# Expert outputs scattered to their tokens' rows in memory and read back, in place of a product with a zero-one matrix

## The reference

```python
p_group = softmax(h @ router_group); pg_top, g_idx = top_k(p_group, 1)
# two best experts inside the chosen group, softmax over their logits
combine = sum(one_hot(expert_id, 16) * (pg_top * w_inner)[..., None], axis=2)
for e in range(16):
    hid = silu(h @ w_gate[e]) * (h @ w_up[e])        # 2048 -> 512
    y = y + combine[..., e:e + 1] * (hid @ w_down[e])  # 512 -> 2048
x = x + y
```

## Time and profile before

| | us |
|---|---|
| median of 3 runs | 2903.97 (2903.62 to 2904.36) |
| profiled execution, device time | 2903.89 |
| its span on the core | 2902.2 |
| PE / DVE / ACT / POOL busy | 2873.0 / 1944.2 / 1648.0 / 95.7 |
| mean DMA rate over the span | 219 GB/s |

### The profile page before, as it was taken

How to read it: one execution, slowest core, us unless ns; L and a number is a source line. 1 busy time by engine, 2 the same in 40 slices (tenths; PEclk the granted TensorE clock), 3 DMA queues, 4 the chain that set the end, 5 groups by cost and what they waited for, 6 DMA issues and landing times.

```text
span 2902.2 us, 40355 instructions
## 1 busy us (share of the span) xinstructions
PE 2873.0 (99%) x16476; PEld 2534.4 (87%) x16476; DVE 1944.2 (67%) x2249; ACT 1648.0 (57%) x1916; POOL 95.7 (3%) x80
## 2 busy tenths in 40 slices
PE   8999999999999999999999999999999999999998
PEld 8989988898778888888999988888899999888887
DVE  6767444535599999999675864555565678555556
ACT  6554444434588888887556544555545655344544
POOL 2212000000000000000000000000000000000000
PEclk9999999999999999999999999999999999999999
DMA  7545566645499999999555555555554545555555
GB/s 270 185 160 169 187 211 235 214 157 170 141 332 366 360 363 356 363 369 313 169 171 175 190 193 184 189 180 182 192 194 156 193 160 187 196 193 181 189 194 189
DMA packets 282103, 636.66 MB, mean 219 GB/s; under 512 B 19081, under 2 KB 32962, under 8 KB 264642
## 3 DMA queue, kind: packets, MB, share of 16 engines
q1 hardware_dynamic: 280450, 628.86, 63.0%
q10 hardware_dynamic: 1184, 4.20, 0.4%
q0 software_dynamic: 288, 1.05, 0.1%
HBM read 626.72 MB, written 7.36 MB: 218 GB/s over the span
## 4 chain that ended last, share of the span: by engine, by line
PE 94%; DVE 3%; ACT 1%; issue 1%; DMA 0%; SPq 0%; POOL 0%; POOLq 0%; ACTq 0%; DVEq 0%
PE pairs L741 16%; PE pairs L743 16%; PE pairs L742 16%; PE pairs L761 10%; PE pairs L763 10%; PE pairs L765 10%; PE pairs L1118 2%; PE pairs L1120 2%; PE pairs L1119 2%; DVE w_lo L2089 2%; PE misc L1236 2%; ACT w_hi L1473 1%; PE misc L908 1%; DVE b_lo L2615 1%; PE misc L981 0%
## 5 line engine op out<-in xcount | busy, mean ns | idle before, releaser
L2089 DVE TENSOR_TENSOR w_lo<-raw,w_hi 128x1024 fp32r<-128x1024 f32 x1072 | 1308.6, 1240 | 796.9 <-ACT w_hi L1473 789.6
L1473 ACT ACTIVATE w_hi<-raw 128x1024 fp32r<-128x1024 f32 x1072 | 1122.3, 1061 | 940.5 <-PE pairs L743 547.2
L761 PE MATMUL pairs<-a_hi,w_hi 128*128 128x256 f32 x1920 | 549.0, 286 | 1.5 <-DVE w_lo L2089 1.5
L763 PE MATMUL pairs<-a_lo,w_hi 128*128 128x256 f32 x1920 | 544.0, 283 | 0.0
L765 PE MATMUL pairs<-a_hi,w_lo 128*128 128x256 f32 x1920 | 544.0, 283 | 0.0
L741 PE MATMUL pairs<-w_hi,a_hi 128*128 128x512 f32 x1280 | 504.7, 394 | 3.6 <-DVE w_lo L2089 1.6
L743 PE MATMUL pairs<-w_hi,a_lo 128*128 128x512 f32 x1280 | 498.5, 389 | 0.0
L742 PE MATMUL pairs<-w_lo,a_hi 128*128 128x512 f32 x1280 | 498.4, 389 | 0.0
L761 PEld LDWEIGHTS pairs<-a_hi,w_hi 128*128 128x128 f32 x1920 | 369.2, 192 | 3.9 <-issue 1.9
L763 PEld LDWEIGHTS pairs<-a_lo,w_hi 128*128 128x128 f32 x1920 | 369.3, 192 | 0.5
L765 PEld LDWEIGHTS pairs<-a_hi,w_lo 128*128 128x128 f32 x1920 | 369.1, 192 | 0.0
(11 more groups left out here) (387 smaller groups left out, 3043.0 us busy)
## 6 DMA issues: line engine op xcount, KB each, us to landing
raw<-in_w_in_dram SPq DMA_DIRECT2D x232, 1024.0 KB, 5.1
raw<-in_w_out_dram SPq DMA_DIRECT2D x84, 1024.0 KB, 5.1
raw<-in_w_down_dram SPq DMA_DIRECT2D x54, 1024.0 KB, 6.2
raw<-in_w_gate_dram SPq DMA_DIRECT2D x51, 1024.0 KB, 5.9
raw<-in_w_up_dram SPq DMA_DIRECT2D x51, 1024.0 KB, 6.7
raw<-in_xattn_wk_dram SPq DMA_DIRECT2D x16, 1024.0 KB, 5.0
raw<-in_xattn_wv_dram SPq DMA_DIRECT2D x16, 1024.0 KB, 5.0
raw<-in_xattn_wq_dram SPq DMA_DIRECT2D x16, 1024.0 KB, 5.0
```

Of the source, the lines that this page charges most:

```text
L761: nc.tensor.matmul(o, w_hi[:, s, q, fs], hi[:, k, :], start=(k == 0 and f % 2 == 0), stop=False, skip_group_check=True)
L763: nc.tensor.matmul(o, w_hi[:, s, q, fs], lo[:, k, :], start=False, stop=False, skip_group_check=True)
L1473: a.activation(w_hi[:, h % HSLOTS], landing(h)[:, 2 * (h % 2):2 * (h % 2) + 2, :], ACT.Copy).then_inc(hi_done, 1)
L2089: v.tensor_tensor(w_lo[:, h % HSLOTS], landing(h)[:, 2 * (h % 2):2 * (h % 2) + 2, :], w_hi[:, h % HSLOTS].bitcast(F32), ALU.subtract).then ...
```

## The change

The product with `place` goes. GpSimd writes the rows of each down unit to memory, each slot's row to its token's row of `y_dram[n]` (one for each quarter n), and slots without a token get a row number past the bound and are dropped. All 256 rows of a quarter are complete after the last group's write. Then GpSimd reads the quarter back, in token order, and DVE adds it to `x` once for each quarter, not once for each group and quarter.

```diff
+        y_dram = [nc.dram_tensor(f"expert_rows{n}", (S + 1, COLS), F32).ap() for n in range(4)]
-        place = rounded("place", 512, [P, TT, S])
-        y_lo_r = rounded("y_low", 1024, [P, TT, COLS])
-        y_hi_r = rounded("y_high", 4608, [P, TT, COLS])
+        y_out = [sc(4608, TT, COLS), sc(1024, TT, COLS)]
+        y_back = sc(0, TT, COLS)
...
                 def turn_pick(g):
...
-                    for s in range(tiles):
+                    for s in range(TT):
                         for T in range(TT):
-                            nc.tensor.matmul(misc[:, 0, s * (PER_GROUP + 1):(s + 1) * (PER_GROUP + 1)],
-                                             pick[:, T, s * P:(s + 1) * P], comb[:, T, g, :],
-                                             start=T == 0, stop=T == TT - 1)
-                    for s in range(tiles):
-                        for T in range(TT):
-                            m = nc.tensor.transpose(misc[:, 1, s * S + T * P:s * S + (T + 1) * P],
-                                                    pick[:, T, s * P:(s + 1) * P], ident[:])
+                            m = nc.tensor.matmul(misc[:, 0, s * COMB:(s + 1) * COMB],
+                                                 pick[:, T, s * P:(s + 1) * P], comb[:, T, g, :],
+                                                 start=T == 0, stop=T == TT - 1)
...
-                def spread_y(g, n):
...
-                    for T in range(TT):
-                        for s in range(tiles):
-                            at = place[:, s, T * P:(T + 1) * P]
-                            nc.tensor.matmul(misc[:, 2 + T, :], at, y_hi_r[:, s, :], start=s == 0, stop=False)
-                            m = nc.tensor.matmul(misc[:, 2 + T, :], at, y_lo_r[:, s, :], start=False,
-                                                 stop=s == tiles - 1)
...
 # GpSimd
+            for gr in range(GROUPS):
+                pool.wait_ge(row_ok, gr + 1)
+                for n in range(4):
+                    sent = (y_even, y_odd)[n % 2]
+                    copied(pool, moe_u(gr, E0 + n))
+                    for T in range(TT):
+                        g.indirect_dma_start(y_dram[n], bass.IndirectOffsetOnAxis(ap=slot_row[gr % 2][:, T:T + 1], axis=0),
+                                             y_out[n % 2][:, T, :], None, bounds_check=S, oob_is_err=False)\
+                         .then_inc(sent, 16)
+                    if gr == GROUPS - 1:
+                        pool.wait_ge(sent, 32 * (2 * gr + n // 2 + 1))
+                        if n:
+                            pool.wait_ge(x_added, n)
+                        pool.dma_start(y_back, y_dram[n][1:S + 1].rearrange("(t p) c -> p t c", p=P))\
+                            .then_inc(y_read, 16)
...
 # ScalarE: place_copy is gone
             def y_copy(g, n):
 
                 done("moe", UNITS_G * g + E0 + n)
-                if 4 * g + n:
-                    act.wait_ge(spread, 4 * g + n)
-                a.activation(y_hi_r[:], pairs[:, n % 2], ACT.Copy).then_inc(y_hi_ok, 1)
+                if 4 * g + n >= 2:
+                    act.wait_ge((y_even, y_odd)[n % 2], 32 * ((4 * g + n) // 2))
+                a.activation(y_out[n % 2], pairs[:, n % 2], ACT.Copy).then_inc(pair_read[n % 2], 1)
...
 # VectorE: y_low is gone; combine() also multiplies the token's number into comb (one more small product)
+            def slot_rows(g):
...
+                s1(v.tensor_scalar(no_row, comb_slot[:, :, 5], 0.0, 4.0 * S, ALU.is_equal, ALU.mult))
+                v.tensor_tensor(slot_row[g % 2], no_row, comb_slot[:, :, 5], ALU.add).then_inc(row_ok, 1)
...
-            def add_spread(g, n):
+            def add_back(n):
 
-                dve.wait_ge(spread, 4 * g + n + 1)
+                dve.wait_ge(y_read, 16 * (n + 1))
                 xs = x[:, :, n * COLS:(n + 1) * COLS]
-                v.tensor_tensor(xs, misc[:, 2:4], xs, ALU.add).then_inc(x_added, 1)
+                v.tensor_tensor(xs, y_back, xs, ALU.add).then_inc(x_added, 1)
...
                     else:
-                        run(3); y_low(g, n - 1); run(1)
+                        run(4)
...
-                        run(3); add_spread(g, n - 1); run(1)
+                        run(4)
+                        if g == GROUPS - 1:
+                            add_back(n - 1)
```

More of the change, by code:

```diff
@@ L29 @@
 EXPERTS = GROUPS * PER_GROUP
+COMB = PER_GROUP + 2
 POOL_WINDOWS = (2, 4, 8, 16)
@@ L167, in program @@
         rsum = tiny(2)
-        comb = tiny(TT * GROUPS * (PER_GROUP + 1)).rearrange("p (t g e) -> p t g e", t=TT, g=GROUPS)
-        comb_slot = tiny(TT * (PER_GROUP + 1)).rearrange("p (t e) -> p t e", t=TT)
+        comb = tiny(TT * GROUPS * COMB).rearrange("p (t g e) -> p t g e", t=TT, g=GROUPS)
+        comb_slot = tiny(TT * COMB).rearrange("p (t e) -> p t e", t=TT)
+        token_i = tiny(TT).bitcast(I32)
+        token_f = tiny(TT)
+        no_row = tiny(TT)
+        slot_row = [tiny(TT).bitcast(I32) for _ in range(2)]
         sq_gain = tiny(8).rearrange("p (t j) -> p t j", t=TT)
@@ L385, in program @@
         hid_mm = sem("hid_mm")
-        y_hi_ok = sem("y_hi_ok")
-        spread = sem("spread")
+        y_odd = sem("y_odd")
+        y_read = sem("y_read")
         x_added = sem("x_added")
@@ L834, in turn_sum @@
                 if N == 4:
-                    pe.wait_ge(x_added, 4 * (GROUPS - 1) + c + 1)
+                    pe.wait_ge(x_added, c + 1)
                     pe.wait_ge(n_lo, n)
@@ L1203, in experts @@
                 unit(pc(U["lru0"]), H["lru0"], 0, mm_features, a_hi, a_lo, need=ready(4),
-                     hooks={1: lambda: spread_y(GROUPS - 1, 3), 3: lambda: turn_sum(4, 3, "moe")})
+                     hooks={3: lambda: turn_sum(4, 3, "moe")})
             route_last()
@@ L1832, in x_low @@
                         act.wait_ge(var_ok, 4)
-                        act.wait_ge(x_added, 4 * (GROUPS - 1) + 3)
+                        act.wait_ge(x_added, 3)
                     low_squares(x, T, junk_low, sq_part)
@@ L1849, in x_top @@
                 def x_top():
-                    act.wait_ge(x_added, 4 * GROUPS)
+                    act.wait_ge(x_added, 4)
                     top_squares(x[:, :, 3 * COLS:4 * COLS], sq_part)
@@ L2438, in _ @@
                     few_low()
-            dve.wait_ge(slots_in, 1)
+            dve.wait_ge(slots_in, 2)
+            v.tensor_copy(token_f, token_i)
             for i in range(4):
@@ L2644, in _ @@
                         if g:
-                            run(3); y_low(g - 1, 3); run(4)
-                            add_spread(g - 1, 3); run(1)
+                            run(8)
                         else:
@@ L2655, in _ @@
                             group_slots()
+                        slot_rows(g)
                     elif i == 2 and g < GROUPS - 1:
@@ L2680, in moe_rest @@
             def moe_rest():
-                y_low(GROUPS - 1, 3)
                 split_lo(4, 2, a_hi, a_lo, "norm0")
@@ L2687, in gained @@
                 dve.wait_ge(gain_in, 16)
-                dve.wait_ge(x_added, 4 * (GROUPS - 1) + j + 1)
+                dve.wait_ge(x_added, j + 1)
                 v.tensor_tensor(xg[j], x[:, :, j * COLS:(j + 1) * COLS],
@@ L2952, in _ @@
                         todo[3].append(moe_rest)
-                        todo[4].append(lambda: add_spread(GROUPS - 1, 3))
+                        todo[4].append(lambda: add_back(3))
                         todo[6].append(lambda: gained(3))
```

31 lines of the change are left out of this document (8 added, 23 removed).

## The result

The changed kernel takes 2908.4 us (median of 20 runs, 2904.7 to 2914.7), the kernel before 2903.7 beside it: ratio 1.0016, 95% interval 1.0010 to 1.0022. It is 4.7 us slower. That is inside what the prediction called no difference, but on the other side of 2903.7 than the forecast of 2901, and outside the 2896 to 2907 of its likeliest case. Eighteen of the runs of before lie within 1.2 us (2903.2 to 2904.4) and one at 2905.9, those of after spread over 10 us, which is itself a sign: their time hangs on something that varies. One run of before (6003.4 us) and one of e12_unawaited (3128.9 us) lie far outside and count in no median here.

The account below looks back on a forecast made before the run. It took TensorE as the bound, DVE and transfers near their limits. Groups 0 to 2 -7, last group's products -3.6, round trip +5.5, transfers +1.5, small DVE work +0.5: -3.1 from 2903.97, say 2901 us; range 2892 to 2912.

Parts of the forecast that it names:

- likeliest case: The forecast's own case: R 10 to 15, transfer ceiling near 372 GB/s; 2896 to 2907 us, chance 0.48.
- What goes: `spread_y` products at 16 places leave TensorE's path, 14.5 us; DVE additions, ACT copies and `turn_pick` buy nothing.
- Groups 0 to 2: Twelve places free 10.9 us of TensorE; a transfer ceiling of 372 GB/s lets 7 of it come home.
- Rival 1: Faster: 372 GB/s is demand, not ceiling, and R is about 11; 10 us gained, 2894 us, chance 0.31.
- A rule against the change: Expert stage: a limit of about 358 GB/s per core would make it transfer-bound already, longer by every byte added.
- The last group: Its four spreads give 3.6 us, but the round trip through memory counts there, as DVE waits in order.
- R: Time from the end of `y_copy` to the landing of the read-back: taken as 12.0 us, from 9.5 to 17.
- What R costs: Last group: first quarter late by R - 8.7, third R - 9.8, others hidden; together 2R - 18.5, 5.5 us.
- hidden unless R passes 13: Last group's fourth quarter: `lru0` turns it after four halves of 2.9 us, so only R above 13 costs.
- Transfers +1.5: Last group: reads and last writes, 2.6 MB, delay weights in flight by 1.5 us, bounds 0 and 4.
- Rivals 2 and 4: Slower: 361 GB/s is all there is, 2914 us; or dropped rows move too, about 2912; together chance 0.10.
- Rival 3: Slower by the round trip: GpSimd's indirect issues take 2 us or more, R = 17; +9, 2913 us, chance 0.11.

Follow-up runs that it names:

- e12_unawaited: Changed kernel with all its transfers, but DVE's addition replaced by a same-size instruction that waits for no read-back (experts' part left out of the output): 2892.5 us.
- e2_no_write: Changed kernel without indirect writes and read-backs, DVE's addition replaced by a same-size instruction without a wait (experts' part left out of the output): 2890.7 us.
- e7_more_traffic: e5_hybrid with one more transfer of 512 KB to memory at each of the 12 places of groups 0 to 2: 2899.9 us.
- e8_late: Changed kernel with the same transfers, but the last group's additions, turns and splits after a read-back stand later, for quarters 0 and 1 one unit: 2900.2 us.
- e5_hybrid: Changed kernel, but the last group keeps the product with the zero-one matrix; groups 0 to 2's rows are read back and added early: 2895.1 us, ratio 0.9971.
- e10_late_one: e8_late with only the first 128 slots of a place sent, one indirect transfer instead of two: 2899.7 us.
- e4_one_issue: Changed kernel with only the first 128 slots of a place sent, one indirect transfer instead of two: 2899.7 us.
- e3_fill: Changed kernel with 26 unused matmuls of 512 columns (5.9 us) before the turn of the last group's first quarter and of its fourth: 2912.2 us.
- e11_plain: Changed kernel, but in the last group each indirect transfer is a plain one of 128 rows, which do not reach their tokens: 2903.0 us.

## Why the prediction went wrong, point by point

- **What goes** (14.5 us of products, the rest worth nothing): right. e2_no_write, which removes them and adds no transfer, gives 13.0. The 1.5 missing may be the small DVE work (a term of 0.5) and weights that TensorE now overtakes: ACT waits 6.2 us for four of their loads there. No run separates the two.
- **Groups 0 to 2, "so I take 372 as the ceiling"**: wrong, 7 us where 10.4 came in this trace. A share of 1.02 does not say that no more can move: at 1.01 it was 388, in e7_more_traffic at 1.03 406. The failed step was to take the rate at a full share for a limit, where TensorE set the demand. Rival 1 had this part right.
- **A rule against the change** (about 358 GB/s): it did not bind, 375 over a group and 406 in a stretch. Another page of the Trainium skill (HBM Reference, section Specifications (TRN2)) says that a core that streams alone gets well above that share, about 425. The traces agree that it gets more; over 61 us the most that was asked for and moved is 406.
- **"The last group", R = 12**: this is the step that failed and that decides. The term was mis-sized: R was 16.6, 12.7 and 16.6 where it counts. Of the first's 4.6 us too many, the read is 2.3 (8.8 for 6.5), the write's landing 1.9 (4.73 for 2.6 + 0.2), the notice 0.5 (0.83 for 0.3), and the issues, where I had looked for the risk, -0.1 (2.26 for 2.4).
- **What R costs**: the formulas have the right places, and give too little. With the measured values the first quarter gives 16.6 - 8.7 = 7.9, the third 12.7 - 9.8 = 2.9, the fourth 16.6 - 13 = 3.6 and the second nothing: 14.4. These R are of the profiled execution of after, which goes with the profiled one of e12_unawaited: 2910.8 - 2892.3 = 18.5, of which 1.1 lies before the last group's down units (leads over before of 10.35 and 11.45). The 17.4 left are 3.0 more than the formulas give. TensorE's waits are 8.1 for the first and 1.8 + 1.3 for the third, as the formulas have it, but 4.6 for the fourth, 1.0 more: "hidden unless R passes 13" should have read 12.
- **The granted clock**, which the sum put at nothing without a word: 1.2 us at the first turn and 1.85 at the fourth in that execution. With the 1.0 that makes 4.05 for the 3.0 missing. The 1.0 too much may be weights: in 1300 to 1400 ACT waits 5.6 us for `in_w_down` in e12_unawaited and 1.0 in after. That is not shown. By the medians waits and clock together cost 15.9, and no trace shows the R of an execution at the median.
- **Transfers +1.5**: 1.0 for writes and 0.9 for reads, near enough.
- **Rivals 2 and 4**: neither came. The groups lasted 135.8 us, and GpSimd's queue moved 5.26 MB, the dropped rows not among them.
- **Rival 3** was the mechanism: R near 17, place `add_back`, waits of DVE of 8 us and more. Its price was worked out as +9 with only 7 us won in groups 0 to 2; with 10.4 it is +5.5, and 4.7 was measured. Two terms were mis-sized with opposite signs, 3.4 us in groups 0 to 2 and 10.4 in the last (15.9 for 5.5); that the time came within 0.3% is luck. I gave this rival 0.11 because I took its bound to need slow issues on GpSimd. A chain of five steps in loaded queues came to 16.6 with issues of 2.26 where the bound had 4.0, because the landing was at its bound (4.73 for 4.5 + 0.2) and the read and the first notice beyond theirs (8.8 for 8, 0.83 for 0.3).

Sum, measured: -13.0 (e2_no_write) + 1.0 + 0.9 + 15.9 = +4.7 from the unrounded medians. It comes out by construction, since each term is the step from one median to the next. Two questions stay open: why the landings of writes and reads vary by 2 to 3 us from one kernel to the next, and why an indirect issue takes 1.0 us at one place and up to 4.55 at another.

## What to carry to other kernels

Price a transfer out to memory and back as a chain, with every link at its value in the loaded stretch where it will run. It pays where its result is due late: here in three groups of four (10.4 us won), and not in the fourth (15.9 lost). In e8_late, trips with 18 us and more from the copy's end to the addition (1307.3 to 1325.2 the shortest) were not waited for. So divide such a change by where the result is due, as e5_hybrid does, before dropping it. Count in what TensorE's clock does after a wait. And a busy share of 1.0 on the DMA engines is no proof of a ceiling: add traffic in one stretch to find it.

## What the runs showed of the hardware that was not expected

- An indirect transfer all of whose rows are dropped moved no bytes but was not free: leaving out 16 of them took 8.7 us off the changed kernel, with 1.3 us a place for the issue and up to 3 us in the landing. In e10_late_one, against e8_late, it took off 0.5 us, and the landing was no shorter.
- Two indirect issues of 128 rows took 2.26 us, two plain ones 1.17. Beside DVE's run of `gained` and `w_lo`, all with two SBUF inputs, single indirect issues took 1.2 to 4.55 us; within a run of `w_lo` alone one took 0.98.
- Three of the four reads of 512 KB landed in 6.8 to 8.8 us beside the weights, in a half-loaded stretch such a read took 4.8 to 5.6. The remaining one, issued at 1326.37 into a stretch in which 94 GB/s moved, took 4.0.
- The granted clock was at its lower level when TensorE's wait of 4.6 us ended (after, 1374.10) and when one of 3.8 did (e4_one_issue, 1321.18). It was still at its upper level at the end of waits of 3.4 (e3_fill, 1326.83) and 2.6 us (e11_plain, 1353.30), and fell 1 to 2 us later. After one of 1.8 (after, 1355.42) it did not fall. Where another engine had fallen behind as well, the lower level cost less than half of what the matmuls grew by (1.2 of 2.6 us).
